# Two elementwise steps on ScalarE instead of VectorE, and the query's norm factor applied to the scores

## The reference

```python
qk  = silu(causal_conv(concat([m_q, m_k]), conv_qk))          # 4 taps, 1024 channels
# mlstm: the weight of key s for query t, per head; a = li - cumsum(log sigmoid f)
w_intra = exp(dmat - m_t[..., None])                           # = exp(min(a_s - max_a_t, 0)) in this kernel
s = einsum('bhtd,bhsd->bhts', q, k) * w_intra
# moba and nsa attention, 12 heads of 64
q = partial_rope(rmsnorm(q, q_g)); k = partial_rope(rmsnorm(k, k_g))
p = softmax(where(mask, einsum('qd,kd->qk', q, k) * 64 ** -0.5, NEG))
# nsa, compressed branch
p_c = masked_softmax(einsum('qd,cd->qc', q, Kc) * 64 ** -0.5, c_end <= t)
```

## Time and profile before

| | us |
|---|---|
| median of three runs | 1177.3 |
| lowest and highest | 1176.02, 1179.41 |
| the profiled execution | 1181.94 |
| its span, first to last instruction | 1180.1 |

### The profile page before, as it was taken

The page is one execution under the profiler, slowest core; times in us unless marked ns, Lnnn a source line. Parts: engine busy times, 40 slices in busy tenths (PEclk is TensorE's granted clock), DMA queues, the critical chain, the costliest instruction groups (busy, mean ns, idle before and its releaser), DMA issues.

```text
span 1180.1 us, 17617 instructions
## 1 busy us (share of the span) xinstructions
PE 1131.2 (96%) x6888; PEld 989.7 (84%) x6888; DVE 741.5 (63%) x1275; ACT 627.6 (53%) x989; POOL 111.7 (9%) x99
## 2 busy tenths in 40 slices
PE   8899989999999899989999999999999989999997
PEld 6788779889988788769899887798988767989885
DVE  4786657555556876667555556667555566775555
ACT  4544655544545535746444545565657446656572
POOL 0324010000000324110000000003000000030000
PEclk8988999999999988999999999999999989999999
DMA  8625235555555425235555555444443445444431
GB/s 295 187 77 165 101 107 195 179 191 185 180 195 168 153 77 170 93 112 190 185 187 188 180 189 186 159 147 139 125 143 107 143 151 161 146 126 132 143 123 56
DMA packets 88959, 181.16 MB, mean 154 GB/s; under 512 B 8669, under 2 KB 19805, under 8 KB 88877
## 3 DMA queue, kind: packets, MB, share of 16 engines
q1 hardware_dynamic: 87437, 175.78, 45.9%
q10 hardware_dynamic: 1440, 4.26, 1.0%
HBM read 178.97 MB, written 1.05 MB: 153 GB/s over the span
## 4 chain that ended last, share of the span: by engine, by line
PE 77%; DVE 13%; ACT 6%; issue 3%; DMA 1%; POOL 1%; DVEq 0%; POOLq 0%; SPq 0%; ACTq 0%
PE bank L754 22%; PE bank L756 21%; PE bank L755 21%; DVE w_lo L1561 2%; PE bank L831 2%; ACT w_hi L1193 2%; PE bank L992 2%; PE bank L869 1%; PE bank L897 1%; DVE vecs L1570 1%; PE bank L1120 1%; DVE xn L1847 1%; PE bank L905 1%; PE bank L906 1%; PE bank L904 1%
## 5 line engine op out<-in xcount | busy, mean ns | idle before, releaser
L1561 DVE TENSOR_TENSOR w_lo<-raw,w_hi 128x1024 fp32r<-128x1024 f32 x296 | 366.3, 1241 | 297.6 <-ACT w_hi L1193 293.9
L1193 ACT ACTIVATE w_hi<-raw 128x1024 fp32r<-128x1024 f32 (+1 forms) x320 | 335.1, 1051 | 240.0 <-PE bank L756 205.7
L754 PE MATMUL bank<-h_hi,w_hi 128*128 128x256 f32 x896 | 262.7, 293 | 3.6 <-DVE w_lo L1561 2.1
L755 PE MATMUL bank<-h_lo,w_hi 128*128 128x256 f32 x896 | 257.5, 287 | 0.0
L756 PE MATMUL bank<-h_hi,w_lo 128*128 128x256 f32 x896 | 257.3, 287 | 0.0
L754 PE MATMUL bank<-w_hi,h_hi 128*128 128x512 f32 (+1 forms) x448 | 183.1, 409 | 5.8 <-DVE h_lo L1580 5.3
L754 PEld LDWEIGHTS bank<-h_hi,w_hi 128*128 128x128 f32 x896 | 176.1, 197 | 8.5 <-DVE w_lo L1561 3.4
L755 PEld LDWEIGHTS bank<-h_lo,w_hi 128*128 128x128 f32 x896 | 176.2, 197 | 0.5
L755 PE MATMUL bank<-w_lo,h_hi 128*128 128x512 f32 (+1 forms) x448 | 176.6, 394 | 0.0
L756 PE MATMUL bank<-w_hi,h_lo 128*128 128x512 f32 (+1 forms) x448 | 176.5, 394 | 0.0
L756 PEld LDWEIGHTS bank<-h_hi,w_lo 128*128 128x128 f32 x896 | 175.9, 196 | 0.0
(11 more groups left out here) (295 smaller groups left out, 1502.2 us busy)
## 6 DMA issues: line engine op xcount, KB each, us to landing
raw<-in_w_in SPq DMA_DIRECT2D x144, 512.0 KB, 3.8
raw<-in_w_ff SPq DMA_DIRECT2D x128, 512.0 KB, 4.0
raw<-in_w_out SPq DMA_DIRECT2D x40, 512.0 KB, 3.2
raw<-in_cmp_w SPq DMA_DIRECT2D x8, 512.0 KB, 4.5
raw<-in_w_in SPq DMA_DIRECT2D x8, 404.0 KB, 3.8
x_sb<-in_x SPq DMA_DIRECT2D x2, 512.0 KB, 7.4
gain<-in_norm_ffn ACTq DMA_DIRECT2D x2, 512.0 KB, 6.5
gain<-in_pre_norm ACTq DMA_DIRECT2D x2, 512.0 KB, 5.0
```

The source lines that it names most:

```text
L754: pe.matmul(out_ap, s_hi, m_hi, start=start, stop=False, **kw)
L755: pe.matmul(out_ap, s_hi, m_lo, start=False, stop=False, **kw)
L1193: act.activation(slot(w_hi, u), slot(raw, u), ACT.Copy).then_inc(hi_ready, 1)
L1561: dve.tensor_tensor(slot(w_lo, u), slot(raw, u), slot(w_hi, u).bitcast(F32), ALU.subtract)\
```

## The change

The exponents' add-and-minimum (`m_rows`) moves from DVE to ACT, as a Relu with scale -1 and the negated column `g_na`, and the exponent then takes the scale -1. The first tap of the convolution moves from DVE's `tensor_scalar` to an ACT copy with a per-channel scale; DVE waits for it (`conv_first`) ahead of its three other taps. The query is only multiplied by its gain (`gained_query`, in the first group ahead of `mean_squares`, in the second behind `refine`), and the factor times 64^-0.5 (`v_rs`) goes as a per-row scale into the operation that adds the mask to the scores and takes the maximum; the exponent on ACT loses its scale. The compressed branch multiplies its scores by the factor in an operation of its own.

```diff
@@ ScalarE
+                    elif kind == "m_rows":
+                        ps = src(s)
+                        act.wait_ge(a_ready, l + 1)
+                        for c in range(2):
+                            h = 2 * s[2] + c
+                            link(act.activation(intra[:, h, 0:T], ps[:, c * T:(c + 1) * T], ACT.Relu, scale=-1.0,
+                                                bias=g_na[:, 0, h:h + 1]))
+                            ins = act.activation(intra[:, h, T:T + P], ps[:, c * T + P:(c + 1) * T], ACT.Relu, scale=-1.0,
+                                                 bias=g_na[:, 1, h:h + 1])
...
+                    elif kind == "conv":
+                        c = s[2]
+                        drained(act, ("proj", 0, l, c // 4, c % 4 // 2))
+                        act.activation(m_qk[:, c, :], conv_in[:, c, 0:T], ACT.Copy, scale=conv_col(l, 0, c)).then_inc(conv_first, 1)
...
-                        act.wait_ge(exponent_ready, 2 * l + u + 1)
-                        act.activation(intra[:, 2 * u:2 * u + 2, :], intra[:, 2 * u:2 * u + 2, :], ACT.Exp).then_inc(intra_exp, 1)
+                        act.activation(intra[:, 2 * u:2 * u + 2, :], intra[:, 2 * u:2 * u + 2, :], ACT.Exp,
+                                       scale=-1.0).then_inc(intra_exp, 1)
@@ VectorE, row_max
+                factor = [SCALE, SCALE]
+                if name[0] == "att1":
+                    v = h if h < 4 else 12 + h % 4
+                    factor = [v_rs[:, i, v:v + 1] for i in range(NT)]
-                link(dve.tensor_tensor_reduce(dst[:, 0:P], ps[:, 0:P], const[:, mask:mask + P], 1.0, LOWEST, ALU.add, ALU.max,
+                link(dve.tensor_tensor_reduce(dst[:, 0:P], ps[:, 0:P], const[:, mask:mask + P], factor[0], LOWEST, ALU.add, ALU.max,
...
-                dve.tensor_scalar(row_nb[:, n % 4, :], mx, -SCALE, None, ALU.mult).then_inc(max_ready, 1)
+                dve.tensor_scalar(row_nb[:, n % 4, :], mx, -1.0, None, ALU.mult).then_inc(max_ready, 1)
@@ VectorE, vectors
+                def gained_query(dst, s0, g):
+                    tt(vec[:, :, dst:dst + 4, :], rv[:, :, s0:s0 + 4, :],
+                       g_vec[:, l, g, :].unsqueeze(1).unsqueeze(1).broadcast_to([P, NT, 4, HD]), ALU.mult)
...
+                    n = v0 + 4
+                    link(dve.tensor_scalar(v_rs[:, :, v0:n], v_r[:, :, v0:n], SCALE, None, ALU.mult))
...
+                        link(dve.tensor_tensor(g_na, Fv, gif[:, :, 0:4], ALU.subtract))
...
+                            gained_query(0, 0, 0)
                             mean_squares(0, 8, 2 * l + 1)
...
                             refine(0, 8, 2 * l + 1)
-                            scaled(0, 0, 4, 0)
...
-                            scaled(20, 12, 4, 2)
+                            gained_query(20, 12, 2)
...
-                    elif kind == "m_rows":
-                        for c in range(2):
...
-                            link(dve.tensor_scalar(intra[:, h, 0:T], ps, g_a[:, 0, h:h + 1], 0.0, ALU.add, ALU.min))
-                            ins = dve.tensor_scalar(intra[:, h, T:T + P], ps[:, P:T], g_a[:, 1, h:h + 1], 0.0, ALU.add, ALU.min)
...
-                        signal(exponent_ready)
@@ VectorE, conv
-                        link(dve.tensor_scalar(acc, conv_in[:, c, 0:T], conv_col(l, 0, c), None, ALU.mult))
+                        dve.wait_ge(conv_first, 8 * l + c + 1)
@@ VectorE, cmp_soft
+                        tt(pc, pc, v_r[:, :, 12:16].unsqueeze(3).broadcast_to([P, NT, 4, NC_CMP]), ALU.mult)
```

More of the change, by code:

```diff
@@ L497, in hybrid_blocks @@
         hid = sb("hid", [P, 2, 2, 16])
-        small = sb("small", [P, 512])
+        small = sb("small", [P, 576])
         rows = sb("rows", [8, 3, T])
@@ L529, in hybrid_blocks @@
         half_neg = few(8)
-        v_ss, v_ms, v_r, v_t = few(NT, NVEC), few(NT, NVEC), few(NT, NVEC), few(NT, NVEC)
+        v_ss, v_ms, v_r, v_t, v_rs = (few(NT, NVEC) for _ in range(5))
         gif, g_e, g_lf, g_F, g_a, m_tok, e_m, m_den = (few(NT, 8) for _ in range(8))
+        g_na = few(NT, 4)
         n_gate = few(NT, 12)
@@ L602, in hybrid_blocks @@
         logf_ready, a_ready, m_ready = sem("logf_ready"), sem("a_ready"), sem("m_ready")
-        conv_done, conv_silu = sem("conv_done"), sem("conv_silu")
-        exponent_ready, intra_exp, intra_masked = sem("exponent_ready"), sem("intra_exp"), sem("intra_masked")
+        conv_first, conv_done, conv_silu = sem("conv_first"), sem("conv_done"), sem("conv_silu")
+        intra_exp, intra_masked = sem("intra_exp"), sem("intra_masked")
         m_col_ready, stabilizer = sem("m_col_ready"), sem("stabilizer")
@@ L1230, in softmax_stage @@
                     slot_p, nb = probs[:, h % 3, :], row_nb[:, n % 4, :]
-                    link(act.activation(slot_p[:, 0:P], slot_p[:, 0:P], ACT.Exp, scale=SCALE,
+                    link(act.activation(slot_p[:, 0:P], slot_p[:, 0:P], ACT.Exp,
                                         bias=nb[:, 0:1], accum_out=row_sum[:, g % 2, r, 0:1]))
-                    act.activation(slot_p[:, P:3 * P], slot_p[:, P:3 * P], ACT.Exp, scale=SCALE,
+                    act.activation(slot_p[:, P:3 * P], slot_p[:, P:3 * P], ACT.Exp,
                                    bias=nb[:, 1:2], accum_out=row_sum[:, g % 2, r, 1:2]).then_inc(exp_ready, 1)
@@ L1316, in _ @@
                         free(act.activation(vecT[:, 2 * u:2 * u + 2, :], src(s)[:, :].rearrange("p (c t) -> p c t", c=2), ACT.Copy), s)
+                    elif kind == "m_rows":
[7 more added lines that the diff above has]
+                                                 bias=g_na[:, 1, h:h + 1])
+                            if c == 1:
+                                free(ins, s)
+                            else:
+                                link(ins)
+                    elif kind == "conv":
+                        c = s[2]
+                        drained(act, ("proj", 0, l, c // 4, c % 4 // 2))
+                        act.activation(m_qk[:, c, :], conv_in[:, c, 0:T], ACT.Copy, scale=conv_col(l, 0, c)).then_inc(conv_first, 1)
                     elif kind == "conv_silu":
@@ L1642, in row_max @@
                 free(dve.tensor_tensor_reduce(dst[:, P:3 * P].rearrange("p (b c) -> p b c", b=2),
-                                              ps[:, P:3 * P].rearrange("p (b c) -> p b c", b=2), seen_, 1.0, LOWEST,
+                                              ps[:, P:3 * P].rearrange("p (b c) -> p b c", b=2), seen_, factor[1], LOWEST,
                                               ALU.add, ALU.max, mx[:, 1:2]), key)
-                dve.tensor_scalar(row_nb[:, n % 4, :], mx, -SCALE, None, ALU.mult).then_inc(max_ready, 1)
+                dve.tensor_scalar(row_nb[:, n % 4, :], mx, -1.0, None, ALU.mult).then_inc(max_ready, 1)
             link(dve.memset(flag[:, :], 1.0))
@@ L1813, in _ @@
                         signal(m_col_ready)
-                    elif kind == "m_rows":
-                        for c in range(2):
-                            h = 2 * s[2] + c
-                            ps = src(s)[:, c * T:(c + 1) * T]
-                            link(dve.tensor_scalar(intra[:, h, 0:T], ps, g_a[:, 0, h:h + 1], 0.0, ALU.add, ALU.min))
-                            ins = dve.tensor_scalar(intra[:, h, T:T + P], ps[:, P:T], g_a[:, 1, h:h + 1], 0.0, ALU.add, ALU.min)
-                            if c == 1:
-                                free(ins, s)
-                            else:
-                                link(ins)
-                        signal(exponent_ready)
                     elif kind == "evac" and s[3] == 6:
```

## The result

The changed kernel took 1185.4 us (median of four runs, 1183.1 to 1188.1) against 1177.5 for the kernel before. The ratio is 1.0056, with a 95% interval of 1.0032 to 1.0079: slower by about half a per cent. The forecast was 1182.8 in a range of 1170 to 1189.

The account below looks back on a forecast made before the run. The prediction took PE as the bound, busy 1131.2 of 1180.1 us. A gain of 1.3 us against losses of 6.5 and 0.2 made 5.4 slower, rounded to 5.5: 1182.8 us, range 1170 to 1189.

Parts of the forecast that it names:

- Part 1: Up to the rope's end: query and row work leaves DVE, most freed time goes to POOL waits; gain 0.65 us a layer.
- Part 2: From the rope to the first `cmp`: nothing taken, with ends of -0.4 and +1.4 us.
- Part 3: Convolution up to `kc_n`: late first taps meet POOL's subtractions; loss 2.6 us in the first layer, 2.0 in the second.
- the walk's own rule of exclusion: POOL and DVE instructions with two SBUF operands exclude each other for a whole instruction; one POOL subtraction takes 2.4 us.
- Part 4: Compressed branch and behind: added operation, scale pointers and chunk 7's first tap make each layer 0.95 us later.
- the sum: Both layers together: gain 1.3 us, losses 6.5 and 0.2; net 5.4 us slower, rounded to 5.5.
- PE's clock falls with the longer waits: Rival: longer stops at the rope and `kc_n` add 6.4 us of slower clock, 1189.2; chance 0.16 with the upper ends.
- the upper ends: Case that more of the terms' higher losses come true; chance 0.16 together with the clock rival.
- The same difference from 1177.3: Step from profiled execution, 4.6 us above the runs' median, to the median: its slowdown applied to 1177.3 gives 1182.8.
- freed VectorE time reaches PE: Rival: DVE's linked steps keep POOL out, rope ends 3.1 us earlier; gain 4.9 us in two layers, 1172.4; chance 0.22.

Follow-up runs that it names:

- e5_conv_early: The changed kernel with ScalarE's first taps of chunks 1 and 2 moved from behind `turn` 3 to ahead of `turn` 2: 1175.8 us, ratio 0.9982.
- e2_conv_only: The kernel before with only the convolution's first tap moved to ScalarE: 1182.6 us, ratio 1.0063.
- e3_rows_only: The kernel before with only the exponents' add-and-minimum (`m_rows`) moved to ScalarE: 1182.2 us, ratio 1.0065.
- a_again: The changed kernel unaltered, run again beside the experiments: 1185.3 us, ratio 1.0070 to the kernel before.
- e4_query_only: The kernel before with only the query's factor moved to the scores: 1175.4 us, ratio 1.0006.
- e1_no_conv: The changed kernel with the convolution's first tap back on VectorE: 1177.3 us, ratio 1.0019.
- e6_rows_late: The changed kernel with `m_rows` 0 one rounding later in ScalarE's list, behind that of p = 13: 1187.4 us, ratio 1.0080.
- e11_combined: e5_conv_early with rests of p = 14, 16, 17 on VectorE, not GpSimd, and chunk 7's ScalarE tap behind those of 5 and 6: 1165.5 us, ratio 0.9899.
- e10_no_pointer: e5_conv_early with the constant 0.125 in place of the pointer to `v_rs` in the mask-and-maximum: 1173.1 us, ratio 0.9971.

## Why the prediction was right, and where it was not

**The sign and its cause.** The forecast said slower by 5.5 us because VectorE would wait for a first tap that stands behind `turn` 3 and a late load. It waited 8.08 us, until 91.68 (forecast 93.5). e5_conv_early, which moves only that, takes the whole loss away, and e2_conv_only, which has only that, has a loss of this size. This is shown. What the forecast did not foresee is that the rows alone, without the query's part, are as slow (e3_rows_only).

**Part 1.** `w_lo` of p = 12 at 47.24 (forecast 47.2) and unstretched: right. `m_rows` on ScalarE: 1.77 us (forecast 1.8); GpSimd's pair at 49.96 (49.9): right. The rope's end was mis-sized: 55.89 against 56.6. The walk let one step pass between GpSimd's two and left five for the end. In fact the first step started at 49.83, before GpSimd, and one more went between, so four were left when GpSimd ended at 54.8. The gain is 1.4 us in each layer instead of 0.65, and 12.9 us from the start of the chain to its end (14.3 before) in a_again too. Of it e4_query_only has 1.2 by itself, and e3_rows_only 0.2.

**Part 2.** The forecast took nothing, with ends of -0.4 and +1.4. The bank's wait of 1.0 us went as said. GpSimd's subtraction for p = 17 came at 70.41 among the small steps, as said. The evacuation began at 74.83 instead of 75.26, and PE waited 1.8 us for it, where it hardly waited before: so the gain of the parts ahead mostly ended there: 0.4 us are left of the 1.4 at the rope. That is the step's own picture, "comes no earlier". The pointer was right (0.06 us). With the rows left on VectorE (e4_query_only) PE waits 0.2 us there.

**Part 3.** `kc_n` ended at 115.92 (its copy's end in the trace) instead of 113.32 in the profile before: 2.6 us, exactly the value taken. In the second layer it ended at 468.85 instead of 464.77, of which 2.2 us were there at the start of the rope's chain: 1.9, against 2.0. That much agreement is partly luck, since the way there was another, and since 2.6 lies below the walk's own lower end (2.2 and 0.5 for the pointers). The maxima began at 97.72, not behind 100.3, because GpSimd began at 90.69 and not 92.55: the whole stretch was earlier, by PE's clock among other things (it was granted 0.65 over 76 to 92 us before and 0.79 after). By the text's own test ("wrong in part 3 if the maxima begin by 98, or if `kc_n` was waited for by no more than now") two marks say wrong: 97.72, and a wait at `kc_n` of 1.8 instead of 2.2 (in the second layer it grew, from 2.1 to 3.2). The delay was real but PE paid it one stage sooner. The step that failed is the reader of the delay: the walk went from the hidden layer straight on to the evacuation and `kc_n`, and passed over the fact that `hidden` holds bank 2, which the unit p = 20 opens. It also had no entry for the 2.33 us of the 30-element step, although the walk's own rule of exclusion covers a late step beside GpSimd's.

**Part 4.** Half of it is shown: the tap's 0.39 us stands in ScalarE's list. That it reaches PE was only argued.

**The layers.** The residual additions behind each mixing part (line, first and last start) tell how far the shift had grown:

```profile
L1602 DVE TENSOR_TENSOR x_sb<-x_sb,bank x8: 678/684/689, 175.9 to 536.5; 128x512 f32<-128x512 f32 x8
```
```profile
L1622 DVE TENSOR_TENSOR x_sb<-x_sb,bank x8: 679/685/689, 177.6 to 540.9; 128x512 f32<-128x512 f32 x8
```

The first is the kernel before, the second the one after: 1.7 us late behind the first layer's mixing part, 4.4 at the end of the second's. The forecast's per-layer sums were about 3.0 and 2.4. Both profiled executions had the same mean clock, 0.974, and differ by 3.8 us in span; so the forecast's 5.4 was too much for the kernel's own work. In span x clock it is 2.3. The convolution, 4.4 in the sum, measured 3.8 to 4.2. The query and the rows, which the sum has as a loss of 1.0 (2.3 for pointers and added operations, less 1.3 at the rope), measured as a gain of 1.7 to 1.9 (e1_no_conv). These are the terms that were mis-sized.

**The clock.** That the total came out higher all the same, and not lower, goes with the rival "PE's clock falls with the longer waits", which the forecast priced at 6.4 us on top and gave 0.16 together with the upper ends. It is the term missing from the sum: 5.4 us in the means of one set. Its mechanism as written, one more slow stretch at the rope and at `kc_n`, is seen in the trace after (0.70 over 55 to 60 us, 1.00 before; 0.68 behind the stop at p = 20), but these come with as many fewer elsewhere: summed over all windows of 5 us both profiled executions have 58 us at the slower clock. One trace each does not show the difference. The means over the runs do (0.9787 against 0.9742 in one set). There was a second slip here. The profiled execution of the kernel before, at 1181.94 and with a clock of 0.974, was a run with an unusually low clock for that kernel (6 of its 94 others have 0.974, none less); the one after, 1185.7, was near its median. "The same difference from 1177.3" was therefore no safe step. Two errors, too much for the work (5.4 against 2.3 of span x clock) and nothing for the clock, met near the right total. That is luck, and the sign and its cause are not.

The rival *freed VectorE time reaches PE* holds for the query part alone (2.9 us of span x clock), and that part got 0.65 a layer in the sum. Its sum takes 1.2 us for the bank, where the earlier trace rows has 1.0. The rule quoted from the Trainium skill (ScalarE: Activation LUTs, "Rules for kernel authors") to keep relu and multiplications on VectorE comes out here in effect, though not by its reason, a price per element in bf16, which no run here shows: moved to ScalarE, the rows cost 1.2 us of span x clock behind the query's part, and the first taps 3.8, but nothing where they stand well.

## What to carry to other kernels

Before a step goes to an engine with more idle time, find its place in that engine's list and ask what is waited for ahead of it. Two first taps a layer were worth 9.5 us by standing behind or ahead of the transposes. Where VectorE has the longer chain, a subtraction of 1.2 us that it makes itself can cost less than one of 2.4 us that GpSimd makes for it, since VectorE stands still for most of the latter: three such moves, with a tap's place, took the ratio from 0.9982 (e5_conv_early) to 0.9899. Follow a delay to every bank that the late step holds, not only to the next step in the list. And before two traces are compared by the times in them, find how far the one runs ahead of the other at a step that no edit touches: in e6_rows_late 1.3 us of that, against the profile after, looked like a gain at the rope.

## What the runs showed of the hardware that was not expected

**Kernels with longer waits of PE tend to have a lower mean clock.** Over the thirteen kernels of the table the clock part rises with the sum of PE's waits: the correlation is 0.83 and the slope 1.0. e11_combined has 21.0 and 20.8, a_again 29.5 and 30.5. But the waits are of one execution each and the clock is a mean. Set against the kernel before of the same set, the correlation is 0.73. With the clock of the profiled execution itself, over all fourteen profiles, it is 0.33: the kernel before has 24.8 us of waits and a clock part of 30.7 there, the one after 28.0 and 30.8. e10_no_pointer lies 3 us off the line. So a price of a stop in clock does not follow from these runs; that waits are the cause is argued, not shown.

**A one-input step on VectorE is held by GpSimd too.** The forecast's rule named VectorE instructions with two SBUF operands. L1877 adds a constant to 30 elements, one operand, and took 2.33 us beside GpSimd against 0.18 alone. The kernel before had shown it already, at GpSimd's subtraction of 63.31 to 65.71, with 2 elements a partition (0.17 us at 78.98):

```profile
64.08 1.66 DVE L1645 TENSOR_SCALAR small<-small 128x2 f32<-128x2 f32 x1
```

In a_again it was the counterpart of this step (L1669), and not the hidden layer's, that GpSimd held (2.29 us), with a stop of 5.5 us behind it. The Trainium skill (SBUF — State Buffer, "SBUF: two separate sides") has this: an instruction in one of the two-port modes takes the lock as well. The trace agrees in that the step was held, by that number; in which mode it ran no row shows. Which of two waiting engines goes next the rows show again: GpSimd's second subtraction let one rope step pass after its first.

**The granted clock moves a kernel by 15 us from run to run.** The 94 runs of the kernel before span 1168.0 to 1182.6 us, with clocks of 0.988 and 0.974 at these ends, while the product of span and clock stays within a standard deviation of about 1.3 us. For kernels that differ by less than 0.5% the product tells more from ten runs than the times do.
